# Decay matrices of a gated delta rule: the column term as the bias of sixteen exponentials per matrix

## What is computed

```python
gc = jnp.cumsum(g, axis=-1)                       # log-decay, summed inside a chunk
incl = jnp.tril(jnp.ones((C, C), bool))
decay = jnp.exp(jnp.where(incl, gc[..., :, None] - gc[..., None, :], -jnp.inf))
a_mat = jnp.where(strict, jnp.einsum('bhnid,bhnjd->bhnij', k_beta, k) * decay, 0.0)
lmat = a_mat + jnp.eye(C)
sol = lax.linalg.triangular_solve(lmat, rhs, lower=True, unit_diagonal=True)
qk = jnp.einsum('bhnid,bhnjd->bhnij', q, k) * decay
```

## Time and profile before

| | |
|---|---|
| runs (us) | 1909.58, 1904.08, 1912.15; median 1909.58 |
| profiled execution, its own time | 1906.97 us |
| its span | 1905.2 us |
| TensorE busy | 1806.2 us (95%) |
| VectorE busy | 847.6 us (44%) |
| ScalarE busy | 576.7 us (30%) |
| GpSimd busy | 72.2 us (4%), 55 instructions |
| mean granted TensorE clock | 0.977 of full |
| the stage of the change | about 860 to 960 us of the span |

### The profile page before, as it was taken

The page is one execution under the profiler, slowest core; times in us unless marked ns, Lnnn a source line. Parts: engine busy times, 40 slices in busy tenths (PEclk is TensorE's granted clock), DMA queues, the critical chain, the costliest instruction groups (busy, mean ns, idle before and its releaser), DMA issues.

```text
span 1905.2 us, 30461 instructions
## 1 busy us (share of the span) xinstructions
PE 1806.2 (95%) x11720; PEld 1406.2 (74%) x11720; DVE 847.6 (44%) x1609; ACT 576.7 (30%) x1032; POOL 72.2 (4%) x55
## 2 busy tenths in 40 slices
PE   7998999989989999799799999999999999999998
PEld 5777999967779999677688877888655555555554
DVE  5956554459465554377833374114222222222222
ACT  2244443312444443255121242302222222222221
POOL 0010000000100000005320000000000000000000
PEclk9989999999999999999899999998999999999999
DMA  7533444545334444332312232345699999999992
GB/s 272 213 131 135 157 175 176 186 168 201 133 133 155 177 176 179 125 113 89 106 45 89 111 111 101 122 166 225 250 398 389 390 403 395 397 392 401 404 391 104
DMA packets 63963, 404.09 MB, mean 212 GB/s; under 512 B 13056, under 2 KB 14592, under 8 KB 15232
## 3 DMA queue, kind: packets, MB, share of 16 engines
q1 hardware_dynamic: 63440, 401.34, 54.7%
q10 hardware_dynamic: 432, 1.51, 0.2%
HBM read 401.39 MB, written 1.44 MB: 211 GB/s over the span
## 4 chain that ended last, share of the span: by engine, by line
PE 86%; DVE 9%; ACT 2%; issue 2%; DMA 1%; SPq 0%; DVEq 0%; ACTq 0%
PE ps L815 23%; PE ps L1365 19%; PE ps L924 12%; PE ps L618 7%; PE ps L1339 5%; PE ps L1355 3%; DVE inv L2276 2%; PE ps L1282 1%; PE ps L1256 1%; DVE big L2341 1%; PE ps L575 1%; DVE big L2053 1%; PE ps L640 1%; PE ps L1307 1%; PE ps L1265 1%
## 5 line engine op out<-in xcount | busy, mean ns | idle before, releaser
L924 PE MATMUL ps<-hn,ring 128*128 128x256 f32 x1152 | 268.3, 386 | 3.6 <-ACT hn L1675 3.6
L924 PEld LDWEIGHTS ps<-hn,ring 128*128 128x128 f32 x1152 | 217.2, 194 | 36.6 <-issue 9.3
L815 PE MATMUL ps<-xhi,wlo 128*128 128x272 f32 x800 | 231.0, 289 | 0.0
L815 PE MATMUL ps<-xhi,whi 128*128 128x272 f32 x800 | 230.0, 287 | 0.0
L2116 DVE TENSOR_TENSOR wlo<-ring,whi 128x2048 fp32r<-128x2048 f32 x76 | 174.1, 2291 | 119.0 <-ACT whi L1545 118.9
L815 PE MATMUL ps<-hn_lo,whi 128*128 128x272 f32 x672 | 194.4, 289 | 0.0
L1365 PE MATMUL ps<-big 128*64 128x512 f32 x816 | 181.8, 594 | 0.0
L1365 PE MATMUL ps<-ring,big 128*64 128x512 f32 x816 | 181.7, 594 | 0.0
L1545 ACT ACTIVATE whi<-ring 128x2048 fp32r<-128x2048 f32 x76 | 145.1, 1909 | 83.0 <-PE ps L815 82.7
L618 PE MATMUL ps<-hn,ring 128*128 128x272 f32 x640 | 157.7, 402 | 6.0 <-DVE hn L2025 5.4
L815 PEld LDWEIGHTS ps<-xhi,whi 128*128 128x128 f32 x800 | 151.4, 189 | 0.0
(11 more groups left out here) (400 smaller groups left out, 2653.3 us busy)
## 6 DMA issues: line engine op xcount, KB each, us to landing
ring<-in_stream SPq DMA_DIRECT2D x277, 1024.0 KB, 5.0
big<-in_stream SPq DMA_DIRECT2D x102, 1024.0 KB, 9.5
h<-in_xT SPq DMA_DIRECT2D x1, 1088.0 KB, 5.0
out_xT<-h SPq DMA_DIRECT2D x1, 1024.0 KB, 4.7
big<-in_consts ACTq DMA_DIRECT2D x1, 896.0 KB, 4.6
cst<-in_consts SPq DMA_DIRECT2D x1, 576.0 KB, 6.0
big<-in_consts ACTq DMA_DIRECT2D x1, 326.5 KB, 5.2
from_blocks<-big SPq DMA_DIRECT2D x1, 256.0 KB, 5.8
```

What stands on the lines that cost most here:

```text
L815: m = mm(out, a[:, at_:at_ + P], b[:, k, :], start=first and i == 0, stop=last and i == 2)
L924: m = mm(ps[:, i % 2, n * T:(n + 1) * T], a, b, start=k == 0, stop=k == DC - 1)
```

## The change

The g_i are no longer added by GpSimd. It makes mask minus g_j for MA and mask plus g_j for MB, four products instead of eight. ScalarE adds the column as the bias of its exponentials. Since a bias is one number for each partition and differs by p and head, each matrix of 128x2048 takes 16 exponentials of 128x128 in place of one. MB needs -g_i, so one more copy of 16 columns, with scale -1, is written to `tiny[:, 0:16]` ahead of the copy of line 1803. The waits for `d_built` go from 4 and 8 to 2 and 4, and the end of a matrix still raises `d_exp` once.

```diff
+            def decay_matrix(m, o):
+
+                act.wait_ge(gb_out, 1)
+                for p in range(2):
+                    for hh in range(GH):
+                        i = f(m[:, p, hh, :], m[:, p, hh, :], ACT.Exp, bias=tiny[:, o + GH * p + hh:o + 1 + GH * p + hh])
+                i.then_inc(d_exp, 1)
...
             act.wait_ge(gb_full, 1)
+            f(tiny[:, 0:16], ps[:, 5, 0:16], ACT.Copy, scale=-1.0)
             f(tiny[:, 32:64], ps[:, 5, 0:32], ACT.Copy).then_inc(gb_out, 1)
...
             conv_act("Q2")
-            act.wait_ge(d_built, 4)
-            f(MA[:, :, :, :], MA[:, :, :, :], ACT.Exp).then_inc(d_exp, 1)
+            act.wait_ge(d_built, 2)
+            decay_matrix(MA, 32)
             conv_in("Q3")
             conv_act("Q3")
-            act.wait_ge(d_built, 8)
-            f(MB[:, :, :, :], MB[:, :, :, :], ACT.Exp).then_inc(d_exp, 1)
+            act.wait_ge(d_built, 4)
+            decay_matrix(MB, 0)
...
             for p in range(2):
                 tt(MA[:, p], low, GB[:, :, p * P:(p + 1) * P], ALU.subtract).then_inc(d_built, 1)
             for p in range(2):
-                pool.wait_ge(d_built, p + 1)
-                tt(MA[:, p], MA[:, p], col(32, p), ALU.add).then_inc(d_built, 1)
-            for p in range(2):
                 tt(MB[:, p], up, GB[:, :, p * P:(p + 1) * P], ALU.add).then_inc(d_built, 1)
-            for p in range(2):
-                pool.wait_ge(d_built, p + 5)
-                tt(MB[:, p], MB[:, p], col(32, p), ALU.subtract).then_inc(d_built, 1)
```

## The result

The changed kernel takes 1914.2 us (median of 20 runs, 1909.96 to 1915.59), the kernel before 1907.75 us on the same chip (20 runs). The ratio is 1.0024 with an interval of 1.0015 to 1.0034, that is +4.6 us (2.9 to 6.5). So it is slower, by less than 0.5%. In the profiled runs the span is 1912.4 us after and 1905.2 before.

A forecast was written before the change was run, and what follows sets the result against it. TensorE held 86% of the chain; ScalarE's stretch without idle before the root of Q2 was to delay the inversion. 0.11 + 0 (MA) + 2.38 (MB) + 0 (GpSimd) = +2.5 us, forecast 1911, range 1904 to 1917.

The forecast's parts named there:

- GpSimd's products, 0 at the end, and TENSOR_SCALAR down to 0.62: Four GpSimd products go: worth 0 at the end; VectorE's Q2 convolution operations fall from 3.09 to 0.62 us, 2.47 earlier.
- The extra copy, +0.11: Second ScalarE copy, of -g, ahead of TensorE's last decay-row product: +0.11 us, bounds 0 and 0.20.
- MA's exponentials hidden: MA's sixteen on ScalarE, +2.98 us, end 0.3 before the copy of Q3, which waits for TensorE: cost 0.
- 0.30 us each: Spacing of biased 128x128 exponentials on ScalarE, taken from the attention's: sixteen take 4.80 us in place of 1.82.
- The rivals at 0.15 and at 0.39: Spacing of ScalarE's exponentials: at 0.15 about +0.1 us, chance 0.10; at 0.39, without overlap, +5.0 us, chance 0.12.
- MB +2.98, of which 2.38 reach the inversion: ScalarE's stretch without idle: root of Q2 2.98 us later, 0.60 of slack, inversion on VectorE 2.38 later.
- TensorE's idle of 2.8 us: TensorE waits about 2.84 us for the root of Q2 before the sum of squares of Q3.
- The rider on the clock: New idle before Q3's sum of squares may drop TensorE's clock: 1.7 us lost, delaying V1 inside 3.29 of idle.
- From 958.7 the chain is TensorE's. The 2.38 us are paid in full: From the inversion on, VectorE and GpSimd work moves as a block, then TensorE's chain: 2.38 us reach the end.
- costs nothing more: A TensorE clock drop after 908.8 delays V1 within an idle of 3.29 us, so the forecast time is unchanged.
- The port worth more: Rival: VectorE operations freed from waiting for GpSimd cancel at most 2.5 us, giving 1909; chance 0.05.
- More expert passes: Rival: changed rounding flips routing so two more expert passes of 15.86 us run, giving 1944; chance 0.02.

The follow-up runs named there:

- MA alone: The change with only MA by sixteen biased exponentials, MB built as in the kernel before, no extra copy: 1909.17 against 1908.06 us, ratio 1.0004.
- double dose: Only MB split, into 32 exponentials of 128x64 in place of 16 of 128x128, against the kernel before: 1915.03 against 1907.66 us, ratio 1.0036.
- MB later: The change with MB's sixteen exponentials moved behind the copy of V1, against the kernel before: 1910.05 against 1907.66 us, ratio 1.0011.
- MB alone: Only MB by sixteen biased exponentials, with the extra copy, MA as in the kernel before: 1914.27 against 1908.06 us, ratio 1.0025.
- second pair: Changed kernel and kernel before, each run once more unedited: 1914.33 and 1907.44, both against 1908.94 us, ratios 1.0033 and 0.9993.

## Why the prediction was right or wrong

The predicted time, 1911, is 3.2 us under the measured median, which lies in the range; "same" (within 0.5%) holds. The predicted +2.5 us lies under the interval of 2.9 to 6.5, so one term is missing. That the time and "same" came out says little about the sum, since a range 13 us wide and a bound of 9.5 us would have held +5 as well. By its steps, with after's times less the 2.97 us by which its copy of GB starts later:

- **GpSimd's products, 0 at the end, and TENSOR_SCALAR down to 0.62:** right. The tiles are clear at 876.9 (forecast 877.4), and the two operations take 0.62 us. The 2.47 us come forward and cover MA; in the first profile of after the exponentials start another 0.66 us earlier, by the clock ahead of them, and so does the copy of Q3, which stays in place in the second (29.17 against 29.25 and 29.20).
- **The extra copy, +0.11:** the two stand 0.06 us apart. Too small to tell from nothing.
- **MA's exponentials hidden:** right, with 0.36 us to spare in both profiles of after. In MA alone nothing was to spare and TensorE waited 0.29 us; as a kernel its ratio is 1.0004 (0.9992 to 1.0016).
- **0.30 us each:** right. (4.79 - 0.39) / 15 = 0.293. The rivals at 0.15 and at 0.39 fall, and with the second the rule of the Trainium skill that spoke against the change (ScalarE: Activation LUTs, rules for kernel authors), which made sixteen 6.5 us. The same page's figures in What ACT_TABLE_LOAD costs gave 0.294, and this trace agrees with those.
- **MB +2.98, of which 2.38 reach the inversion:** the root moved by 2.86, the slack in front of the inversion took 0.35 to 0.56, and the DMA is no longer waited for. Measured in the stage: +1.9 and +2.9, mean +2.4, or 2.7 to 2.9 between profiles that start alike. The double dose shows about one for one (3.3 us for 2.98), and MB later and MA alone show nothing else in the stage that costs more than a few tenths.
- **TensorE's idle of 2.8 us:** 2.85. The rider on the clock was right for one execution: V1 took 1.69 us longer in the first profile of after and was absorbed by the shorter idle behind it. In the second, and in MB alone, V1 took its 7.07 us and the query products 5.47 and 5.46, as before.
- **"From 958.7 the chain is TensorE's. The 2.38 us are paid in full", and the clock "costs nothing more":** this step failed. The chain is TensorE's, but its clock is not the same afterwards. The term that was missing is +2.4 and +3.4 us in the two pairs of profiles, of which, in the second pair, 1.46 were seen in one place, 161 us behind the stage, and 1.7 in another, 205 us behind it. I had asked what the delay does to the clock only at the next projection, and took all later work as a fixed length.
- **The port worth more:** not here; V1's convolution is 14.15 us with and without the change. It is worth 6.6 us as soon as GpSimd's two key scalings beside that convolution go, which the change left in place.
- **More expert passes:** no; the expert phase has the same length in all profiles (545.8 to 546.2 us).

Open: why the later grants follow the place of the first product on the raster of the clock. The sorting holds for all fourteen profiles, but it is a sorting and not a test. The runs show that the loss isn't caused by the program's length, by the number of exponentials or by a longer stage as such. How often the drop near 205 us occurs in either kernel is open too, with two profiles of each.

## What to carry over

Splitting one exponential of 128x2048 into sixteen with a bias column costs ScalarE about 2.9 us; that is free where the engine waits for something anyway and is paid in full in a stretch without idle, so look for the place first, and only then at what the moved work relieves. What relieves nobody in its present place (GpSimd's products here) is worth nothing, while the same kind of move beside an operation that shares GpSimd's port gained 6.6 us of path. And where TensorE bounds the kernel, a change of a few us upstream, a delay or a gain, can cost as much again or nothing, by drops of the granted clock far behind it: compare the time behind the stage by itself before calling it moved as a block.

## What was not expected of the hardware

- TensorE's granted clock, 160 us and more behind the changed stage, differs between kernels that run the same instructions there at the same distance: 1.00 or 0.83 in the window at 158 us, with 945.5 to 946.7 or 948.9 to 949.3 us for the whole rest. Both profiles of each of the two kernels agree on it. In all fourteen profiles it goes with the place of the first product on the raster on which the recorded clock changes, 0.03 to 0.29 of a step or 0.62 to 0.98.
- A half-clock stretch can fall on one neighbour or the other at no loss: behind the same idle of 2.85 us, one execution of after had V1 in 8.76 us, 1.60 of idle and the query products in 3.84, and the other V1 in 7.07, 3.28 of idle and the query products in 5.47.
- V1's convolution on VectorE took 14.15 us beside GpSimd's scalings (two of the keys, in four products, and one of the queries), 7.86 beside that of the queries alone, and 3.60 beside none of them. V2's, with GpSimd idle, took 2.71: the same six instructions, up to five times as long.
